# Re-ordering the second block's mixer: output chunks between the transforms of the long convolution, earlier constant loads, the attention norm beside the filter spectra

## The reference, cut to what matters

```
q, k, v, f, hy = split_projection(h @ w_in)
a  = neighbourhood_attention(q, k, v, kc, vc, rpb)            # 1024 channels
fo = fft2(f, over tokens and channels).real                  #  512 channels
u  = dwconv_centred(hy); v, x1, x2 = split(u)                 #  3 x 512 channels
filt = rfft(mlp(pos; w1, w2, w3) * decay)                     # filter spectra, orders 0 and 1
z  = x1 * (irfft(rfft(v) * filt[0]) + v * bias[0])            # long convolution, order 0
y  = x2 * (irfft(rfft(z) * filt[1]) + z * bias[1])            # long convolution, order 1
m  = concat(rmsnorm(a, g), rmsnorm(fo, g), rmsnorm(y, g))
x  = x + g1 * (m @ w_out)
...
```

## Time and profile before

| | |
|---|---|
| median of three runs | 2642.92 us |
| the profiled execution | 2647.48 us |
| its span in the trace | 2645.7 us |
| mean granted TensorE clock over the span | 0.991 of full speed |
| PE busy | 2586.6 us, 98% of the span |
| DVE busy | 1912.6 us, 72% |
| ACT busy | 1182.7 us, 45% |
| moved by DMA | 558.24 MB, 211 GB/s on average |

### The profile page before, as it was taken

The page is one execution under the profiler, slowest core; times in us unless marked ns, Lnnn a source line. Parts: engine busy times, 40 slices in busy tenths (PEclk is TensorE's granted clock), DMA queues, the critical chain, the costliest instruction groups (busy, mean ns, idle before and its releaser), DMA issues.

```text
span 2645.7 us, 49893 instructions
## 1 busy us (share of the span) xinstructions
PE 2586.6 (98%) x20904; PEld 2497.6 (94%) x20904; DVE 1912.6 (72%) x2449; ACT 1182.7 (45%) x1257; POOL 0.2 (0%) x4
## 2 busy tenths in 40 slices
PE   7999999999999999999999999989899999999998
PEld 7988999999999999999999899948899999999997
DVE  8788887987898888888893236756666666666667
ACT  5766554444644444444442234333444444444443
POOL 0000000000000000000000000000000000000000
PEclk9999999999999999999999999999999999999999
DMA  8666667776888888888863254322455565555553
GB/s 293 216 233 213 224 224 254 250 246 222 295 272 285 282 281 281 278 284 283 274 227 100 93 175 145 128 86 97 159 191 194 196 196 195 193 191 192 192 192 111
DMA packets 282425, 558.24 MB, mean 211 GB/s; under 512 B 10279, under 2 KB 16712, under 8 KB 281928
## 3 DMA queue, kind: packets, MB, share of 16 engines
q1 hardware_dynamic: 282104, 553.60, 62.5%
q10 hardware_dynamic: 144, 2.10, 0.2%
HBM read 553.56 MB, written 2.10 MB: 210 GB/s over the span
## 4 chain that ended last, share of the span: by engine, by line
PE 90%; DVE 6%; issue 2%; ACT 1%; DMA 1%; SPq 0%; DVEq 0%; ACTq 0%
PE PS L1691 77%; PE PS L1701 3%; PE PS L1703 3%; PE PS L1702 3%; DVE WL L918 2%; PE PS L2017 1%; PE PS L2028 1%; PE PS L2035 1%; PE PS L1751 1%; DVE ada1c L1174 1%; PE PS L1917 0%; PE PS L1850 0%; ACT WH L493 0%; DVE X L1288 0%; PE PS L1953 0%
## 5 line engine op out<-in xcount | busy, mean ns | idle before, releaser
L493 ACT ACTIVATE WH<-RAW 128x1024 fp32r<-128x1024 f32 x840 | 888.2, 1060 | 1308.4 <-PE PS L1691 1189.6
L918 DVE TENSOR_TENSOR WL<-RAW,WH 128x1024 fp32r<-128x1024 f32 x840 | 1017.1, 1222 | 606.5 <-ACT WH L493 599.7
L1691 PE MATMUL PS<-XL,WH 128*128 128x256 f32 x4288 | 667.6, 278 | 0.0
L1691 PE MATMUL PS<-XH,WH 128*128 128x256 f32 x3752 | 589.2, 279 | 4.4 <-DVE WL L918 2.4
L1691 PE MATMUL PS<-XH,WL 128*128 128x256 f32 x3752 | 581.9, 277 | 0.0
L1691 PEld LDWEIGHTS PS<-XL,WH 128*128 128x128 f32 x4288 | 572.4, 189 | 0.0
L1691 PEld LDWEIGHTS PS<-XH,WH 128*128 128x128 f32 x3752 | 501.2, 189 | 7.9 <-issue 4.6
L1691 PEld LDWEIGHTS PS<-XH,WL 128*128 128x128 f32 x3752 | 498.8, 189 | 0.0
L1691 PE MATMUL PS<-HH,WH 128*128 128x256 f32 x1728 | 269.1, 278 | 1.4 <-DVE FR L1275 0.8
L1691 PE MATMUL PS<-HH,WL 128*128 128x256 f32 x1728 | 267.4, 277 | 0.0
L1691 PE MATMUL PS<-HL,WH 128*128 128x256 f32 x1728 | 267.4, 277 | 0.0
(11 more groups left out here) (270 smaller groups left out, 1955.7 us busy)
## 6 DMA issues: line engine op xcount, KB each, us to landing
RAW<-in_w_ff SPq DMA_DIRECT2D x128, 1024.0 KB, 6.1
RAW<-in_w_in SPq DMA_DIRECT2D x112, 1024.0 KB, 5.2
RAW<-in_w_up SPq DMA_DIRECT2D x88, 1024.0 KB, 5.0
adab<-in_ada_w SPq DMA_DIRECT2D x128, 512.0 KB, 5.4
RAW<-in_w_down SPq DMA_DIRECT2D x44, 1024.0 KB, 5.1
ada1b<-in_ada_w SPq DMA_DIRECT2D x64, 512.0 KB, 6.1
RAW<-in_w_out SPq DMA_DIRECT2D x32, 1024.0 KB, 5.1
RAW<-in_w_oa SPq DMA_DIRECT2D x8, 1024.0 KB, 5.2
```

Of the source, the lines that this page charges most:

```text
L493: A(WH[:, c.base % 2, hs], RAW[:, c.base % SLOTS, hs], ACT.Copy).then_inc(hi_done, 1)
L918: tt(WL[:, b, hs], RAW[:, c.base % SLOTS, hs], WH[:, b, hs].bitcast(f32), ALU.subtract)\
L1691: ins = MM(out[:, f, :], w[:, b, kk, f * P:(f + 1) * P], x, start=first and n == 0 and f % 2 == 0, stop=last and n == 2, skip_group_check= ...
```

## The change

It moves work within the four queues. No matmul, no vector instruction and no transfer is added or dropped.

- SP: pz, w1h, w2h, fcl and fcd wait for `2 * (C_OUT2 - 2)` halves, two chunks sooner; dec and Ef still wait for `2 * C_OUT2`. For this pz, w1h and w2h get another place. The chunks of `w_out` are loaded in the order of OUT2_ORDER.
- The chunks of group 1 with row quarters 0, 1 and 2 are computed before (0, 3). Chunk (0, 0) stands between `inverse(0)` and `to_tokens(1)`, chunks (0, 1) and (0, 2) between `forward(1)` and `inverse(1)`, (1, 0) before `norm_sum(N_H)`, (1, 1), (1, 2) and (0, 3) after it.
- `norm_sum(N_A)` stands after the second filter; root, scaling and rounding of the attention's quarters follow beside the spectra.
- `inverse(1)` writes banks 4 and 5 and no longer banks 2 and 3; the sums of squares and the Fourier results use other banks too.
- Chunk C_OUT2 + 1 is converted later: on ACT after `to_tokens(0)`, on DVE after hSD.

```
-SUM_BANK = [4, 4, 4, 7, 0, 2, 4, 4, 4]
+SUM_BANK = [4, 4, 4, 7, 1, 0, 6, 4, 4]
+OUT2_ORDER = [(0, 0), (0, 1), (0, 2), (1, 0), (1, 1), (1, 2), (0, 3), (1, 3)] + [(g, s) for g in (2, 3) for s in range(4)]
+OUT2_LAST = [max(n for n, (g, _) in enumerate(OUT2_ORDER) if g == k) for k in range(4)]
...
-        pz = at("pz", [33, T], 110 * K + 192)
+        pz = at("pz", [33, T], 85 * K + 192)
...
-            sp.wait_ge(pe_half, 2 * C_OUT2)
+            for t in range(SLOTS):
+                out2_load(t)
+
+            sp.wait_ge(pe_half, 2 * (C_OUT2 - 2))
             sp.dma_start(pz[:, :], d["pz"]).then_inc(sm["mlp_in"], 16)
...
             sp.dma_start(fcd[:, :, :], d["fcd"]).then_inc(sm["four_in"], 16)
+            sp.wait_ge(pe_half, 2 * C_OUT2)
             sp.dma_start(dec[:, :, :, :], d["dec"]).then_inc(sm["e_in"], 16)
...
 (ScalarE)
             high(Place(C_OUT2))
+            for t in (40, 41, 42):
+                attention2_step(t)
+            act.wait_ge(sm["a2_done"], HEADS)
+            for n in range(2):
+                A(SM[:, 4 * n:4 * n + 4, :], q2[:, 4 * n:4 * n + 4, :], ACT.Square).then_inc(sm["mix_sq"], 1)
+            fourier_tokens(0)
+            sine(0)
+            fourier_tokens(1)
+            fourier_tokens(2)
+            fourier_tokens(3)
+            fourier_channels(0)
+            fourier_channels(1)
+            sine(1)
+            fourier_channels(2)
+            fourier_channels(3)
+            root(N_A, 1024)
             to_tokens(0)
+            high(Place(C_OUT2 + 1))
             for n in range(5):
                 spectrum(n)
+            group_high(N_A, 0)
+            group_high(N_A, 1)
             for n in range(5, 10):
                 spectrum(n)
-            root(N_A, 1024)
+            root(N_F, 512)
+            group_high(N_F, 2)
             to_tokens(1)
...
 (VectorE)
             low(Place(C_OUT2))
             attention2_step(40)
-            low(Place(C_OUT2 + 1))
-            for t in range(41, 44):
-                attention2_step(t)
-                short_conv(2, t - 41)
             sine_argument(0)
+            short_conv(2, 0)
+            short_conv(2, 1)
             sine_argument(1)
+            short_conv(2, 2)
+            dve.wait_ge(sm["mix_sq"], 2)
+            add_squares(SM, 1, True)
...
             inverse_root(N_F)
             scaled(SM, fY[:, :, :], lambda k: col("mix", k), 2)
+            gated_output(0)
+            low(Place(C_OUT2 + 2))
+            dve.wait_ge(sm["zf_ps"], 2)
             split_low(E_OUT2, XH, XL, quarter(SM, 2), 2)
+            products(1)
+            low(Place(C_OUT2 + 3))
+            low(Place(C_OUT2 + 4))
             gated_output(1)
...
 (TensorE)
+            pe.wait_ge(sm["ks_done"], 9)
+            norm_sum(N_F, SM)
             pe.wait_ge(sm["gi_in"], 16)
             inverse(0)
-            pe.wait_ge(sm["ks_done"], 10)
-            norm_sum(N_A, SM)
+            pe.wait_ge(sm["norm_rt"], N_F + 1)
+            out2(0, True)
             to_tokens(1)
             forward(1)
-            norm_sum(N_F, SM)
-
-            pe.wait_ge(sm["norm_rt"], N_A + 1)
-            wide(Place(C_OUT2), Place(Q_OUT2), 0, e=E_OUT2)
-            pe.wait_ge(sm["norm_rt"], N_F + 1)
+            out2(1, True)
+            out2(2, True)
             inverse(1)
-            wide(Place(C_OUT2 + 1), Place(Q_OUT2), 1, e=E_OUT2)
+            out2(3)
             norm_sum(N_H, SM)
-            wide(Place(C_OUT2 + 2), Place(Q_OUT2), 2, e=E_OUT2)
-            wide(Place(C_OUT2 + 3), Place(Q_OUT2), 3, e=E_OUT2)
+            out2(4)
+            out2(5)
+            out2(6, True)
```

More of the change, by code:

```diff
@@ L457, in _ @@
             sp.dma_start(Gi[:, :, :], d["gi"]).then_inc(sm["gi_in"], 16)
-            for g in range(1, 4):
-                wide(Place(C_OUT2 + 4 * g), w_out2, g * NB)
+            for t in range(SLOTS, 4 * SLOTS):
+                out2_load(t)
             def ff2_step(j):
@@ L806, in sine, with fourier_channels @@
                 A(hdn[:, n, :], sr[:, 0, :], ACT.Sin).then_inc(sm["mlp_sin"], 1)
-            high(Place(C_OUT2))
-            attention2_step(40)
-            high(Place(C_OUT2 + 1))
-            for t in range(41, 44):
-                attention2_step(t)
[L813 to L821, removed]
+            def fourier_channels(n):
                 act.wait_ge(sm["fy_ps"], n + 1)
[L823 to L827, removed]
+                A(fY[:, n, :], bank(6 + n % 2)[:, 0:T], ACT.Copy).then_inc(sm["fy_done"], 1)
             def spectrum(n):
@@ L1506, in _ @@
             own.settle()
+            low(Place(C_OUT2 + 1))
             def products(o):
@@ L1536, in gated_output @@
                     own.did(stt(tmp[:, k, :], src[:, k, :], col("hy_bias", HT * o + k),
-                                bank(2 + k // 2)[:, (k % 2) * T:(k % 2 + 1) * T], ALU.mult, ALU.add))
+                                bank(2 + 2 * o + k // 2)[:, (k % 2) * T:(k % 2 + 1) * T], ALU.mult, ALU.add))
                 own.settle()
                 tt(dst[:, 0:HT, :], tmp, gate, ALU.mult).then_inc(sm["hz_done"], 1)
-            products(0)
-            dve.wait_ge(sm["mix_sq"], 2)
-            add_squares(SM, 1, True)
+            inverse_root(N_A)
+            for n in range(2):
+                scaled(SM, quarter(q2, n), lambda k: col("mix", k), n)
             dve.wait_ge(sm["fy_done"], FNG)
@@ L1547, in _ @@
             folded(SM, 2)
-            gated_output(0)
-            inverse_root(N_A)
-            for n in range(2):
-                scaled(SM, quarter(q2, n), lambda k: col("mix", k), n)
             for n in range(2):
                 split_low(E_OUT2, XH, XL, quarter(SM, n), n)
-            products(1)
+            products(0)
             inverse_root(N_F)
             scaled(SM, fY[:, :, :], lambda k: col("mix", k), 2)
+            gated_output(0)
+            low(Place(C_OUT2 + 2))
+            dve.wait_ge(sm["zf_ps"], 2)
             split_low(E_OUT2, XH, XL, quarter(SM, 2), 2)
+            products(1)
+            low(Place(C_OUT2 + 3))
+            low(Place(C_OUT2 + 4))
             gated_output(1)
@@ L1577, in residual2 @@
                 ins.then_inc(acc_free[q.slot], 1)
[L1579 removed]
+            for t in range(7, 4 * SLOTS):
                 low(Place(C_OUT2 + t))
[L1581 removed]
+                if t == 7:
                     gain_of(0, 4 * KC, "norm2")
[L1583 to L1584 removed]
+                if t - 2 in OUT2_LAST:
+                    residual_squares(C_OUT2, Q_OUT2, OUT2_LAST.index(t - 2), residual2)
                 if t in (10, 14):
@@ L1989, in to_tokens, with filters @@
                     ins.then_inc(sm["zt_ps"], 1)
-            pe.wait_ge(sm["mlp_sin"], 2)
-            pe.wait_ge(sm["mlp3_in"], 16)
-            for n in range(4):
+            def filters(n):
                 o, t = n // 2, n % 2
```

74 lines of the change are left out of this document (38 added, 36 removed).

## The result

| | before | changed |
|---|---|---|
| median of four runs on one chip | 2642.23 us | 2623.41 us |
| lowest to highest | 2640.18 to 2643.03 | 2622.78 to 2628.11 |
| ratio | 1 | 0.9927, 95% interval 0.9915 to 0.9939 |
| profiled execution, its span | 2647.48, 2645.7 us | 2622.78, 2620.9 us |

The change saves 18.8 us, 0.7%; 2623.9 had been forecast. The page has the same work as before and 12.7 us less of it on PE, with as many instructions: 9.1 us of it lie in the stage that was re-ordered, mostly matmuls that no longer run at the lower clock, and 3.5 ahead of it.

What follows compares the result with a forecast made beforehand. PE, busy 98%, bounds the kernel; only its waits and lower-clock time can be won. Terms 6.3 + 1.8 - 0.6 - 0.6 + 5.2 + 1.5 + 3.4 + 0.8 = 17.8, taken as 19.0: 2623.9 us, range 2618.5 to 2630.

Steps and rivals of the forecast that it cites:

- Constants: Before and in the token transforms: constants come 10 us sooner, waits for w2h and fcd and a clock fall go, 6.3 us.
- fY: Fourier mix and MLP: PE's wait for fY goes, covered by the last two token transforms, 1.8 us gained.
- w3h: Before the filters, now earlier: w3h lands late and PE waits for it, 0.6 us lost.
- Filters and spectra: PE waits 0.4 us before the third filter and 0.9 before the first spectrum, where it waited 0.7: 0.6 us lost.
- `products(0)`: DVE's queue before `products(0)`, around `forward(0)`: the added work there costs 0, with 2 us of cover.
- zT and its fall: Behind `inverse(0)`: a chunk covers the 2.6 us wait, the 2.8 clock fall goes, zt's wait grows to 0.9: 5.2 us.
- YS: Before `inverse(1)`: two chunks cover DVE's work on quarter 2 and `products(1)`, so the wait goes, 1.5 us.
- N_H: After the last norm's sum: two chunks cover the path to quarter 3; XL's 1.8 wait and 1.6 fall go, 3.4 us.
- Tails: Over the stage: each of five removed waits also gives back a last matmul's 0.16 us tail, 0.8 us.
- rival 1: The clock still falls once, at `forward(1)` or behind the 0.9 us wait before the spectra: 2626.7 us, chance 0.18.
- 2 and 3: Rivals: w3h lands late and the clock falls, 2628.7, chance 0.07; another SP transfer holds the constants, 2630.2, chance 0.05.
- Rival 5: From filters to the end of `inverse(0)` the clock stays at 0.50: 22 us slower than before, 2665 us, chance 0.04.

Runs made afterwards that it cites:

- second profile of before: The kernel before, run again with nothing edited, one execution: 2642.68 us, stage 178.0 us.
- front-half kernels: The kernel before with constants sooner and the front re-ordered, back half left: 2640.33 us; the same with the channel transforms' banks also changed: 2634.48 us.
- quarter 3 sooner: The changed kernel with chunk (0, 3) ahead of (1, 2): median 2628.63 us, ratio 0.9951; again, one execution, 2627.60 us.
- YS uncovered: The changed kernel with chunks (0, 1) and (0, 2) behind `inverse(1)`, two low-part conversions on DVE moved later: 2635.08 us, ratio 0.9964.

## Why the prediction was right, term by term

The forecast was 2623.9 and the median is 2623.4; its likeliest case is the one that came, and by the mechanism that it gave: the waits that it named go, and the falls of the clock behind them. By its own sum:

- **Constants, 6.3.** Right in size: 6.1 to 7.0 of stage when they are taken away from the finished kernel. Alone they bring 5.3 of the median, within noise of that; in that profile the next thing to be late (the sine, 1.4 us) took some, and the clock fell later instead.
- **fY, 1.8.** Gone, and with the re-ordered front alone too, so the cover that was named holds. The runs add a condition that the prediction nowhere named: without banks 6 and 7 the re-order brings a wait of 3.1 us in the place of fY's. The step that was missing is which bank's release stands ahead of the channel transforms.
- **w3h, -0.6.** Wrong, 0. It was issued at 1714.5, 1.0 us after the stage's start, and the forecast had 1.2. It landed in 9.8 us, not 11.9 to 14.1, at 1724.3, and the filters came at 1727.13. I had taken off only the 0.64 MB in front of it; dec and Ef, beside it, landed faster too, in 5.2 and 7.6 us where they had taken 8.0 and 12.3.

```profile
dec<-in_dec SPq DMA_DIRECT2D x1, 1024.0 KB, 5.2
Ef<-in_ef SPq DMA_DIRECT2D x1, 768.0 KB, 7.6
...
w3h<-in_hy_w SPq DMA_DIRECT2D x1, 512.0 KB, 9.8
```

- **Filters and spectra, -0.6.** +0.2: PE waits 0.49 us for hSD in all and waited 0.74; the 0.4 before the third filter did not occur.
- **`products(0)`, 0 with 2 us of cover.** Right, with more: the split ends 1.2 us before `forward(0)` does (the idle time in the row), where I had 0.6, and the products, 7.3 us long, are through at 1759.9 for an `inverse(0)` at 1761.4.

```profile
1749.54 1.82 DVE L976 TENSOR_TENSOR XL<-SM,XH 128x512 fp32r<-128x512 f32 x2
1752.57 1.23 DVE L1528 TENSOR_TENSOR pp<-PS,KS 128x1024 f32<-128x1024 f32 x1 [1.21 <-PE PS L2032]
```

- **zT and its fall, 5.2.** Right: 4.9 when undone. The wait for zt is 0.74, not 0.9. The sum left out that the fall had already reached the transposes, which took 1.32 us then and 1.04 now: 0.3.
- **YS, 1.5.** Gone. With the whole cover undone the stage is 11.6 longer.
- **N_H, 3.4.** The wait is gone. Its 1.6 of fall belonged to that one execution: behind the same wait the second profile of before has none, nor have those of the front-half kernels. The path from the sum's start to quarter 3 is 1814.57 - 1806.48 = 8.1 us in the second profile with quarter 3 sooner; I had 9.6. That came from 7.3 in the kernel before and a conversion more. In the trace the path before was 8.8 (1815.10 to 1823.93: the sum and the wait of 0.47 for WL belong to it), with two conversions on DVE while ACT formed the root; the one conversion now lies mostly beside ACT's rounding and so lengthens it little.

```profile
1806.48 0.67 PE L1773 MATMUL PS<-SM,mats 128*128 128x256 f32 x2
...
1814.57 1.11 PE L1702 MATMUL PS<-XH,WH 128*128 128x256 f32 x4 [1.76 <-DVE XL L976]
```

- **Tails, 0.8**, were not measured apart. With the w3h and hSD terms put right the sum is 17.8 + 0.6 + 0.8 = 19.2, against 20.8 in the pair of profiles that it was made from. Of the other 1.6 the traces show about 1.5: the ninth wait, 0.5; the fall in the transposes, 0.3; seven tails and not five, 0.3; and 98 chunk matmuls fewer at the slower rate (last section), 0.4.

That the median was hit to 0.5 us is in part chance. The sum was made against a profiled execution that was 5 us over its median, of which about 3 were falls of the clock (and 0.2 of a wait) that the second profile doesn't have, while the forecast fell short of that pair by 1.8. The two errors nearly cancel.

Of the rivals, 1 (a fall stays at `forward(1)`), 2 and 3 did not come: no window of the changed kernel's stage is below 1.00, in either of its profiles. Rival 5, the clock at half speed through the transforms, has nothing for it. On rival 1: in every profile in which the transposes of zT stand behind a chunk and not behind a wait (the changed kernel twice, and its variants with late constants, with YS uncovered, with the attention's norm late and with quarter 3 sooner, twice) `forward(1)` takes 7.13 us behind a wait of 0.74. With a wait of 2.6 to 3.0 in front of them it fell in all six. So without the wait there is no fall; what the Trainium skill says of transposes (TensorE: Matmul & The Clock Gate, Part 4: PE-mode transpose) cost nothing in seven profiles. Whether the transposes help the clock to fall where a wait stands in front of them isn't shown: all six had both, and the one wait of such a length with a chunk behind it, 3.4 us for the root, brought no fall.

## What to carry to other kernels

When independent work is laid over a wait on the engine that bounds, ask first what that work itself needs: the chunk behind `inverse(0)` covers 2.6 us only because the attention's norm is summed before the spectra and not behind `inverse(0)`, and the re-ordered front pays only because its outputs moved to banks that nobody else holds. Undo parts of a change from the finished kernel as well as adding them to the old one: what a part gives shows in which waits go and which come in their place, while the sizes from single profiles (4 us for the constants one way, 6 to 7 the other) hold falls of the clock and a rate of the chunks that differ between executions. And where a wait of 0.7 to 3 us may bring a fall of the clock, look at a second profile before the fall is booked as a gain.

## What the runs showed of the hardware that I had not expected

**A fall of the clock behind a short wait is a matter of the execution.** Behind zT (2.6 to 3.0 us) it came in six profiles of six, behind fcd in three of three. Behind XL (1.6 to 2.0 us) it came in two of seven, behind hSD (0.74 us) in three of five: in the three kernels with the constants sooner and the back half as before, and in neither profile of the kernel before. Behind hyC (3.1) and before `inverse(1)` with YS uncovered (8.6) it came in the one profile of each. Behind fY (1.8) it came in none of three, behind YS (1.5) in none of five, behind the root, 3.4 us, not in the one profile. The length of the wait alone doesn't decide. The Trainium skill (TensorE: Matmul & The Clock Gate, Part 1: The HAM clock gate) says that the number of slow matmuls at a kernel's start is "run-variable"; the runs here show the same of falls in its middle. What decides between two executions of one kernel stays open.

**Two rates at one clock.** At a granted clock of 1.00 four matmuls of a chunk come every 0.47 us in some stretches and every 0.45 to 0.46 in others. Two rows each from 1807 on, of the changed kernel and of its second profile:

```profile
1807.54 0.62 PE L1702 MATMUL PS<-XH,WL 128*128 128x256 f32 x4
1807.99 0.62 PE L1702 MATMUL PS<-XH,WH 128*128 128x256 f32 x4
```
```profile
1807.53 0.64 PE L1702 MATMUL PS<-XH,WL 128*128 128x256 f32 x4
1808.00 0.63 PE L1702 MATMUL PS<-XH,WH 128*128 128x256 f32 x4
```

Between 1803 and 1833 the first has 9 such steps of 0.47 or more and the second 53. A step is 0.018 us longer at that rate, so 44 x 0.018 = 0.8 us. Counted one by one over the whole stage, 99 of 761 chunk matmuls come at the slower rate (0.118 us apart, not 0.113) in the first and 289 in the second, which makes 0.9; the stages differ by 0.8. PE waits for nothing there and PEclk is 1.00; the cause stays open. It sets how small a gain a single pair of profiles can show here.
